# Three of four expert rows of a mixture layer added by TensorE, the fourth by VectorE

## The reference, cut to what matters

```python
s = jnp.einsum('thpd,hpnd->thpn', q, sub_keys)
s1, i1 = lax.top_k(s[:, :, 0], PEER_TOPK)
s2, i2 = lax.top_k(s[:, :, 1], PEER_TOPK)
cand_s = (s1[..., :, None] + s2[..., None, :]).reshape(n, PEER_H, PEER_TOPK * PEER_TOPK)
cand_i = (i1[..., :, None] * PEER_NKEYS + i2[..., None, :]).reshape(n, PEER_H, PEER_TOPK * PEER_TOPK)
top_s, pos = lax.top_k(cand_s, PEER_TOPK)
idx = jnp.take_along_axis(cand_i, pos, axis=-1)
gates = jax.nn.softmax(top_s, axis=-1)
act = jax.nn.gelu(jnp.einsum('chkd,cd->chk', u_tab[i_c], x_c))
return jnp.einsum('chk,chkd->cd', g_c * act, v_tab[i_c])
```

## Time and profile before

| | |
|---|---|
| median of 3 runs | 3675.85 us (3671.82 to 3684.18) |
| the profiled execution | 3676.11 us, its span 3674.3 us |
| mean granted TensorE clock over the span | 0.88 |
| the gather stage | from about 566 to 1260 us |

### The profile page before, as it was taken

The page is one execution under the profiler, slowest core; times in us unless marked ns, Lnnn a source line. Parts: engine busy times, 40 slices in busy tenths (PEclk is TensorE's granted clock), DMA queues, the critical chain, the costliest instruction groups (busy, mean ns, idle before and its releaser), DMA issues. The chain is left out here.

```text
span 3674.3 us, 52170 instructions
## 1 busy us (share of the span) xinstructions
PE 3066.0 (83%) x21162; PEld 2559.3 (70%) x21162; DVE 2384.8 (65%) x4291; ACT 1260.9 (34%) x2037; POOL 586.1 (16%) x321
## 2 busy tenths in 40 slices
PE   7977765666655599888999988999997999997899
PEld 4856652222211299778989886998986898987798
DVE  3677747888888777365768726777726775544554
ACT  1043211111111233354343445344345334343643
POOL 1010024444445300400000050000040000031000
PEclk9988776777767799979999987999998999996999
DMA  8932229999999886414858531867652764542153
GB/s 337 392 123 94 99 88 380 379 366 378 381 390 385 335 321 246 180 47 168 324 184 345 222 139 47 349 231 304 260 188 73 292 252 173 186 182 91 47 195 126
DMA packets 123103, 854.19 MB, mean 232 GB/s; under 512 B 17300, under 2 KB 18580, under 8 KB 21012
## 3 DMA queue, kind: packets, MB, share of 16 engines
q1 hardware_dynamic: 85748, 582.69, 41.4%
q0 software_dynamic: 36864, 268.45, 18.3%
q10 hardware_dynamic: 288, 0.26, 0.0%
HBM read 850.24 MB, written 1.11 MB: 232 GB/s over the span
## 5 line engine op out<-in xcount | busy, mean ns | idle before, releaser
L268 PE MATMUL ps<-h_hi,w_hi 128*128 128x256 f32 x3328 | 956.5, 287 | 53.0 <-DVE h_lo L459 25.9
L193 DVE TENSOR_TENSOR w_lo<-w_ring,w_hi 128x2048 fp32r<-128x2048 f32 x284 | 650.0, 2290 | 473.6 <-ACT w_hi L188 471.7
L269 PE MATMUL ps<-h_lo,w_hi 128*128 128x256 f32 x3328 | 951.9, 286 | 0.0
L270 PE MATMUL ps<-h_hi,w_lo 128*128 128x256 f32 x3328 | 951.6, 286 | 0.0
L188 ACT ACTIVATE w_hi<-w_ring 128x2048 fp32r<-128x2048 f32 x330 | 629.6, 1913 | 658.1 <-PE ps L270 640.9
L268 PEld LDWEIGHTS ps<-h_hi,w_hi 128*128 128x128 f32 x3328 | 645.0, 194 | 63.4 <-DVE h_lo L459 28.9
L269 PEld LDWEIGHTS ps<-h_lo,w_hi 128*128 128x128 f32 x3328 | 645.4, 194 | 3.2
L270 PEld LDWEIGHTS ps<-h_hi,w_lo 128*128 128x128 f32 x3328 | 644.8, 194 | 0.0
L2909 PE MATMUL ps<-expert_rows,expert_diag 128*128 128x512 f32 x512 | 382.4, 891 | 283.7 <-ACT expert_diag L2947 283.7
L193 POOL TENSOR_TENSOR w_lo<-w_ring,w_hi 128x2048 fp32r<-128x2048 f32 x46 | 212.3, 4633 | 2192.2 <-ACT w_hi L188 2192.2
L2909 PEld LDWEIGHTS ps<-expert_rows,expert_diag 128*128 128x128 f32 x512 | 121.1, 260 | 540.5 <-ACT expert_diag L2947 437.9
(11 more groups left out here) (454 smaller groups left out, 3980.4 us busy)
## 6 DMA issues: line engine op xcount, KB each, us to landing
w_ring<-in_w_stream SPq DMA_DIRECT2D x376, 1024.0 KB, 4.8
a_ring<-in_a_stream SPq DMA_DIRECT2D x108, 1024.0 KB, 7.2
a_ring<-in_t_stream SPq DMA_DIRECT2D x36, 1024.0 KB, 10.0
a_ring<-in_m_stream SPq DMA_DIRECT2D x8, 1024.0 KB, 7.3
alibi<-in_alibi SPq DMA_DIRECT2D x3, 2048.0 KB, 8.5
cond_row<-in_cond_row SPq DMA_DIRECT2D x8, 512.0 KB, 3.9
expert_rows<-in_experts,expert_idx POOLq DMA_INDIRECT x256, 9.2
gates<-mod_rows SPq DMA_DIRECT2D x3, 1024.0 KB, 5.8
```

The source lines that it names most:

```text
L193: pool.tensor_tensor(self.w_halves(n)[1], self.w_item(n), self.w_halves(n)[0], ALU.subtract).then_inc(self.lo_made, 1)
L268: pe.matmul(out, stationary[0], moving[0], start=start, stop=False)
L269: pe.matmul(out, stationary[0], moving[1], start=False, stop=False)
L270: return pe.matmul(out, stationary[1], moving[0], start=False, stop=stop)
```

## The change

Of every four expert rows, VectorE adds the one with n % 4 = 0 (the first row of an even batch) and TensorE the other three. So in an even batch the work is split as before, and in an odd batch TensorE adds both rows and VectorE none. ScalarE makes a diagonal for each row of TensorE, so two in an odd batch; `expert_diag` has a place for each row and grows from 4 to 8 matrices of 128 x 128. The counts of the waits follow: `diagonal` and `pe_freed` count expert rows of TensorE (192), `dve_freed` those of VectorE (64), and GpSimd waits for the one that freed the slot. The order of the engines' work is otherwise the same.

```diff
--- before.py
+++ after.py
@@ -2793,6 +2793,16 @@
 EXPERTS = TT * PEER_PAIRS
 BATCHES = EXPERTS // PER_BATCH
 UNIT = TT * PEER_TOP
+DVE_EVERY = 4
+
+
+def rows_of_dve(n):
+
+    return -(-n // DVE_EVERY)
+
+
+def rows_of_pe(n):
+    return n - rows_of_dve(n)
 
 
 HEADS_AHEAD = 3
@@ -2840,7 +2850,7 @@
         rows = core.sb(ctx, "expert_rows", [P, G_SLOTS, 2 * D])
         dot = core.sb(ctx, "expert_dot", [P, G_BATCHES, PER_BATCH])
         coef = core.sb(ctx, "expert_coef", [P, G_BATCHES, PER_BATCH])
-        diag = core.sb(ctx, "expert_diag", [P, G_BATCHES, P])
+        diag = core.sb(ctx, "expert_diag", [P, G_BATCHES, PER_BATCH, P])
         acc = core.sb(ctx, "expert_sum", [P, TT, D])
         block = ctx.enter_context(nc.Block())
 
@@ -2864,9 +2874,11 @@
                 if n % UNIT == 0:
                     pool.wait_ge(listed.sem, listed.at(n // UNIT + 1))
                 if n >= G_SLOTS:
-                    used = (n - G_SLOTS) // PER_BATCH + 1
-                    by = pe_freed if slot % PER_BATCH else dve_freed
-                    pool.wait_ge(by.sem, by.at(used))
+                    before = n - G_SLOTS
+                    if before % DVE_EVERY:
+                        pool.wait_ge(pe_freed.sem, pe_freed.at(rows_of_pe(before + 1)))
+                    else:
+                        pool.wait_ge(dve_freed.sem, dve_freed.at(rows_of_dve(before + 1)))
                 at = n % UNIT
                 pool.indirect_dma_start(rows[:, slot, :], None, core.io["experts"],
                                         bass.IndirectOffsetOnAxis(ap=idx[:, n // UNIT, at:at + 1], axis=0)).then_inc(
@@ -2902,15 +2914,18 @@
                 score(h)
             opened = set()
             for b in range(BATCHES):
-                n = PER_BATCH * b + 1
-                t = tile_of(n)
-                pe.wait_ge(diagonal.sem, diagonal.at(b + 1))
-                for half in range(2):
-                    last = pe.matmul(core.y[:, 2 * t + half, :], diag[:, b % G_BATCHES, :],
-                                     rows[:, n % G_SLOTS, D + half * BANK:D + (half + 1) * BANK],
-                                     start=t not in opened, stop=n // UNIT == PEER_H - 1 and n % PEER_TOP == PEER_TOP - 1)
-                opened.add(t)
-                last.then_inc(pe_freed.sem, 1)
+                for n in range(PER_BATCH * b, PER_BATCH * (b + 1)):
+                    if n % DVE_EVERY == 0:
+                        continue
+                    t = tile_of(n)
+                    pe.wait_ge(diagonal.sem, diagonal.at(rows_of_pe(n + 1)))
+                    for half in range(2):
+                        last = pe.matmul(core.y[:, 2 * t + half, :], diag[:, b % G_BATCHES, n % PER_BATCH, :],
+                                         rows[:, n % G_SLOTS, D + half * BANK:D + (half + 1) * BANK],
+                                         start=t not in opened,
+                                         stop=n // UNIT == PEER_H - 1 and n % PEER_TOP == PEER_TOP - 1)
+                    opened.add(t)
+                    last.then_inc(pe_freed.sem, 1)
                 if b in HEADS_LATER:
                     score(HEADS_LATER[b])
 
@@ -2943,9 +2958,11 @@
                     raise_gates(RAISED[b])
                 act.wait_ge(weighed.sem, weighed.at(b + 1))
                 if b >= G_BATCHES:
-                    act.wait_ge(pe_freed.sem, pe_freed.at(b - G_BATCHES + 1))
-                act.activation(diag[:, b % G_BATCHES, :], core.ident[:], ACT.Copy,
-                               scale=coef[:, b % G_BATCHES, 1:2]).then_inc(diagonal.sem, 1)
+                    act.wait_ge(pe_freed.sem, pe_freed.at(rows_of_pe(PER_BATCH * (b - G_BATCHES + 1))))
+                for e in range(PER_BATCH):
+                    if (PER_BATCH * b + e) % DVE_EVERY:
+                        act.activation(diag[:, b % G_BATCHES, e, :], core.ident[:], ACT.Copy,
+                                       scale=coef[:, b % G_BATCHES, e:e + 1]).then_inc(diagonal.sem, 1)
                 if b in HEADS_LATER:
                     copy_q(HEADS_LATER[b])
 
@@ -3049,17 +3066,19 @@
                 at = n % UNIT
                 dve.wait_ge(acts.sem, acts.at(b + 1))
                 dve.tensor_tensor(c, c, gates[:, n // UNIT, at:at + PER_BATCH], ALU.mult).then_inc(weighed.sem, 1)
+                if n % DVE_EVERY:
+                    return
                 dve.wait_ge(weighed.sem, weighed.at(b + 1))
-                if b:
-                    dve.wait_ge(dve_freed.sem, dve_freed.at(b))
+                if n:
+                    dve.wait_ge(dve_freed.sem, dve_freed.at(rows_of_dve(n)))
                 t = tile_of(n)
                 dve.scalar_tensor_tensor(out=acc[:, t, :], in0=rows[:, n % G_SLOTS, D:2 * D], scalar=c[:, 0:1],
                                          in1=acc[:, t, :], op0=ALU.mult, op1=ALU.add).then_inc(dve_freed.sem, 1)
 
             def finish(t, batches):
 
-                dve.wait_ge(pe_freed.sem, pe_freed.at(batches))
-                dve.wait_ge(dve_freed.sem, dve_freed.at(batches))
+                dve.wait_ge(pe_freed.sem, pe_freed.at(rows_of_pe(PER_BATCH * batches)))
+                dve.wait_ge(dve_freed.sem, dve_freed.at(rows_of_dve(PER_BATCH * batches)))
                 for half in range(2):
                     part = slice(half * BANK, (half + 1) * BANK)
                     last = dve.tensor_tensor(acc[:, t, part], acc[:, t, part], core.y[:, 2 * t + half, :], ALU.add)
...
```

More of the change, by code:

```diff
@@ L3096, in peer_stage @@
         s.passed(16 * EXPERTS // G_SLOTS)
-    for s in (dots, acts, weighed, diagonal, dve_freed, pe_freed):
+    for s in (dots, acts, weighed):
         s.passed(BATCHES)
+    dve_freed.passed(rows_of_dve(EXPERTS))
+    for s in (diagonal, pe_freed):
+        s.passed(rows_of_pe(EXPERTS))
 class Modulation:
```

## The result

| | before | after |
|---|---|---|
| median of 7 runs | 3678.09 us | 3697.5 us |
| lowest to highest | 3671.13 to 3684.18 | 3686.95 to 3702.26 |
| profiled execution | 3676.11 us, span 3674.3 | 3701.32 us, span 3699.5 |

A forecast was written before the change was run, and what follows sets the result against it. DMA bounds plain batches, VectorE the choice stretches, ScalarE and TensorE the block after batch 4. Terms -2.0 + 0.8 - 6.4 + 2 + 2 = -3.6 us gave 3672 us; range 3650 to 3698.

The forecast's parts named there:

- choice stretches: Stretches where VectorE also computes the next head's choice and sets the pace; only their excess, some 60 us, can be won.
- interval from 15: From batch 15's sum to the next unit's first, under a choice: 1.28 us gained per unit, not in unit 0.
- intervals 3, 4: From the sums of batches 3 and 4: 1.28 us gained after 3, less 0.85 for batch 3's rows delaying batch 4's.
- interval 5, units 0 to 4: From batch 5's sum: gains nothing, since VectorE already waits 0.86 us for ScalarE there.
- block: TensorE's next-head queries and scores after batch 4, units 0 to 4: batch 5's rows wait behind, costing 2.49 us each.
- what the gather keeps in units 5, 6: Units 5 and 6, choice without queries: the gather keeps 4.5 us of 8.0 and 7.4, gaining 3.2 each.
- plain batches and last unit: 72 batches without a choice, bound by the DMA: late slots charged 2 us, bounds 0 and 20.
- end: Closing addition waits for TensorE's last five rows: 1.2 us later, 4.8 with two rows slow; +2 us taken.
- rival 2: Late slots at the low clock lengthen plain batches by 0.32 us each, 23 us in all: 3693 us, chance 0.25.
- Rival 1: All 22 odd intervals under a choice gain 1.28 us, the lag goes in full: 28 us, 3648 us, chance 0.20.
- Rival 3: TensorE at the low clock throughout becomes the bound, 0.70 us a batch, 50 us: 3720 us, chance 0.05.
- The clock: TensorE's clock rises within an odd batch's burst (5.7 us) and is lost in about half the pauses before odd batches.

The follow-up runs named there:

- e1_drop: Kernel before without VectorE's sums of odd batches; their first rows are left out, slots come free at the weighing: 3661.44 us, ratio 0.9966.
- e5_fill: Changed kernel plus two idle TensorE matmuls after even batches' rows, except where queries and scores follow: 3685.59 us, ratio 1.003.
- e8_only1: Kernel before with only batch 1's first row moved to TensorE in units 0 to 6: 3675.83 us, ratio 0.9996.
- e3_block5: Changed kernel, but VectorE adds the first row of batch 5 in units 0 to 4 again: 3689.22 us, ratio 1.0042.
- e10_fillblock5: Changed kernel with idle TensorE matmuls after even batches, and VectorE keeping batch 5's first row in units 0 to 4: 3674.9 us, ratio 0.9994.

## Why the prediction was wrong

The step that failed is the value of VectorE's freed time in the choice stretches. The prediction let the whole 1.28 us of the interval from 15 count, where VectorE already waited for the DMA, and it let that of interval 3 count too, with late releases charged at only 0.85 us in five units. The runs show that the first could give nothing and that the second was taken back by batch 1's late release: -7.7 us forecast and +3.5 measured, -4.7 forecast and +4.9 measured. Its sum and the profiles side by side, in us (the forecast's terms sorted into the columns of the table):

| | forecast | measured |
|---|---|---|
| interval from 15 | 6 x -1.28 = -7.7 | +3.5 |
| interval 1 | 7 x -1.28 = -9.0 | -9.3 |
| intervals 3, 4 | -9.0 + 5 x 0.85 = -4.7 | +4.9 |
| interval 5, units 5 and 6 | -2.6 | 0.0 |
| interval 5, units 0 to 4 | 0 | -2.1 |
| block | 5 x 2.49 = +12.5 | +14.6 |
| what the gather keeps in units 5, 6 | +3.8 | +2.2 |
| plain batches and last unit | +2 | +4.3 |
| end | +2 | +1.7 |
| sum | -3.7 (-3.6 there, by rounding) | +19.8 |

Seven of the nine lines hold within some 2.6 us. The two others make 21 of the 23 us between forecast and result.

*The interval from 15* was counted at 1.28 us gained per unit. In the timeline of before, unit 4, VectorE waits in that very interval:

```profile
920.66 1.22 DVE L3042 CUSTOM_DVE_ANT_0 expert_rows<-expert_rows,h 128x1024 f32<-128x1024 f32 x1 [1.20 <-DMA expert_rows<-in_experts,expert_idx]
```

The removed 1.28 us lie ahead of a wait of 1.20, so at most 0.08 could be won. The prediction had used this rule for the plain batches and for batch 5 (where it is right), not here: it took a stretch as VectorE's whose first interval is still the DMA's. e1_drop confirms it: 46.1 against 46.3 without any late release. In the changed kernel the removed sum has turned into waiting; here the interval is 936.89 - 929.28 = 7.61, with waits of 1.13 and 1.25:

```profile
929.28 0.15 DVE L3068 TENSOR_TENSOR expert_coef<-expert_coef,expert_gates 128x2 f32<-128x2 f32 x1
...
930.57 1.23 DVE L3059 CUSTOM_DVE_ANT_0 expert_rows<-expert_rows,h 128x1024 f32<-128x1024 f32 x1 [1.13 <-DMA expert_rows<-in_experts,expert_idx]
...
933.05 1.23 DVE L3059 CUSTOM_DVE_ANT_0 expert_rows<-expert_rows,h 128x1024 f32<-128x1024 f32 x1 [1.25 <-DMA expert_rows<-in_experts,expert_idx]
...
936.89 0.14 DVE L3068 TENSOR_TENSOR expert_coef<-expert_coef,expert_gates 128x2 f32<-128x2 f32 x1
```

and in other units up to 9.18. The 3.5 us that the interval costs over the units are gone in e5_fill, so they too are late releases at the low clock.

*Intervals 3 and 4.* The mechanism was rival 2's, late slots that starve the gather, but the prediction put it into the plain batches only and held that a flight can shorten where VectorE sets the pace. The timeline of after, three intervals later in the same unit:

```profile
944.33 7.91 PE L2923 MATMUL ps<-expert_rows,expert_diag 128*128 128x512 f32 x12 [3.02 <-ACT expert_diag L2964]
...
948.38 0.94 POOL L2883 DMA_INDIRECT expert_rows<-in_experts,expert_idx  x1 [5.86 <-PE ps L2923]
...
955.34 7.11 PE L2923 MATMUL ps<-expert_rows,expert_diag 128*128 128x512 f32 x12 [3.10 <-ACT expert_diag L2964]
...
956.57 1.23 DVE L3059 CUSTOM_DVE_ANT_0 expert_rows<-expert_rows,h 128x1024 f32<-128x1024 f32 x1 [0.58 <-DMA expert_rows<-in_experts,expert_idx]
...
962.59 1.23 DVE L3059 CUSTOM_DVE_ANT_0 expert_rows<-expert_rows,h 128x1024 f32<-128x1024 f32 x1 [1.01 <-DMA expert_rows<-in_experts,expert_idx]
```

Batch 1's burst starts after a pause of 3 us; its first row needs 4 us, GpSimd idles 5.86 us until 948.38, and then four issues follow close together. VectorE waits for the rows of batches 5 and 6 that come of it. Over the seven units interval 3 takes 4.25 to 5.47 us, 3.58 to 4.05 in e5_fill, 4.90 before. The half of the low-clock delay that the sum charged (0.85) was thus the wrong cause and too small: it was for batch 3's rows running into batch 4's, whose slots are filled for batch 8, while the rows that VectorE waits for in interval 3 go into batch 1's slots. e8_only1, which moves batch 1's row alone, has the same loss in 3 and 4 (80.6). e1_drop (late releases gone) and e5_fill (clock up) remove it by two different ways.

*The block* was right in place and cause, and 2.9 us in place of 2.49 a unit; e3_block5 and e10_fillblock5 take it away. *Plain batches*: 5.03 us an interval before, 5.10 after, in the 42 intervals 9 to 14, so they cost some 4 us and not the 23 of rival 2. Rival 2 as written therefore fell, though its time came out, which is luck: its 21 us were spent elsewhere. Rival 1 fell with e1_drop. Rival 3 did not happen: the granted clock is 0.87 and 0.90, not 0.50. *The clock*: I had expected it to be lost in half of the pauses before odd batches, and that was right: 29 of 64 pairs run at the full clock throughout. But where it is low it is low at a burst's start, in batch 1 in all seven units, and the first row frees the slot that GpSimd, which waits in order, needs first. The rule that the prediction took from the Trainium skill ("TensorE: Matmul & The Clock Gate", "HAM oscillation"), that bursts parted by waits for DMA start throttled, agrees with such bursts; it doesn't hold for all of them, as the 29 of 64 show that ran at full speed.

*The end*: the last wait grew from the 1.54 us of the earlier trace rows.

```profile
1275.92 5.42 PE L2923 MATMUL ps<-expert_rows,expert_diag 128*128 128x512 f32 x12 [1.73 <-ACT expert_diag L2964]
...
1281.38 1.28 DVE L3084 TENSOR_TENSOR expert_sum<-expert_sum,ps 128x512 f32<-128x512 f32 x2 [4.57 <-PE ps L2923]
```

From the last weighing to this addition 4.7 us pass, 3.0 before.

Open: why the idle work costs the kernel before 10 us, and why e3_block5 is worth 14 us in its profile, 8 between the medians and 4 by the ratios.

## What to carry to other kernels

In this kernel, work taken off an engine shortened an interval only by what exceeded the wait that the engine already had in that same interval; read this interval by interval, not by stretch. Where buffers are released in order, ask of every move of work who frees the buffer afterwards, and how late at that engine's lowest clock, above all right behind another engine's long block. Move only the pieces that gain, and put work that is due anyway into the pauses ahead of the time-critical matmuls: that took 3654 us where the wholesale move took 3697 (the split of the queries without any moved row: 3663).

## What the runs showed of the hardware

Idle matmuls on TensorE, 1.88 to 3.15 us in a pause, raised the granted clock of two stretches from 0.87 and 0.90 to 1.00 and made the changed kernel 9 to 12 us faster; in the kernel before the same kind of work made it 10 us slower. Two rows of four records each took 3.70 us at the full clock, and in the changed kernel up to 6.69 where it was low at the start. Of four transfers issued close together after an idle stretch of the queue (948.38 to 953.49) the second arrived 5.8 us after its issue and the last 9.1 (953.49 to 962.59); the first row issued behind the block came in 6.3 (974.11 to 980.45).
